# Seven more weight pairs in the Strassen-like form, with even and odd tiles as its halves and the sums over x made ahead

## What is computed

```python
x = x + 0.5 * swiglu_ffn(rms_norm(x, norm_g[i, 0]), ffn_w_gu[i, 0], ffn_w_down[i, 0])
h = rms_norm(x, norm_g[i, 1])
...
x = x + 0.5 * swiglu_ffn(rms_norm(x, norm_g[i, 2]), ffn_w_gu[i, 1], ffn_w_down[i, 1])
```

## Time and profile before

| | us |
|---|---|
| runs of the kernel | 2163.83, 2163.85, 2165.5; median 2163.85 |
| the profiled execution | 2163.63 |
| its span, first to last instruction | 2161.8 |
| TensorE busy | 2144.5 |
| VectorE busy | 1680.9 |
| ScalarE busy | 1176.7 |
| GpSimd busy | 253.0 |

### The profile page before, as it was taken

The page is one execution under the profiler, slowest core; times in us unless marked ns, Lnnn a source line. Parts: engine busy times, 40 slices in busy tenths (PEclk is TensorE's granted clock), DMA queues, the critical chain, the costliest instruction groups (busy, mean ns, idle before and its releaser), DMA issues.

```text
span 2161.8 us, 33546 instructions
## 1 busy us (share of the span) xinstructions
PE 2144.5 (99%) x13412; PEld 1835.3 (85%) x13412; DVE 1680.9 (78%) x2546; ACT 1176.7 (54%) x1922; POOL 253.0 (12%) x187
## 2 busy tenths in 40 slices
PE   9999999999999999999999999999999999999999
PEld 6989897777779898989899997777789898977777
DVE  8789697988678796888787787777688886966873
ACT  6536264667556263546355356777555362638672
POOL 3000004000040000040010112000130000030000
PEclk9999999999999999999999999999999999999999
DMA  7454535131135555354554542222135545332211
GB/s 214 123 136 99 151 94 161 40 98 60 46 89 141 124 137 151 84 162 125 176 129 127 122 126 92 77 75 95 50 79 150 137 100 150 98 131 74 79 59 39
DMA packets 249451, 237.75 MB, mean 110 GB/s; under 512 B 4984, under 2 KB 245240, under 8 KB 249296
## 3 DMA queue, kind: packets, MB, share of 16 engines
q1 hardware_dynamic: 208336, 210.25, 30.3%
q0 software_dynamic: 40752, 25.11, 8.7%
q10 hardware_dynamic: 208, 0.24, 0.0%
HBM read 213.79 MB, written 6.32 MB: 102 GB/s over the span
## 4 chain that ended last, share of the span: by engine, by line
PE 91%; DVE 4%; ACT 2%; issue 1%; DMA 0%; SPq 0%; ACTq 0%; DVEq 0%
PE ps L1982 90%; PE ps L1986 1%; DVE sb_wlo L1334 1%; DMA sb_raw<-ffn_w_gu 0%; ACT sb_whi L771 0%; DVE sb_gla_ek L1689 0%; DVE sb_gla_eq L1692 0%; ACT sb_hyb_th L771 0%; ACT sb_lnb L771 0%; DVE sb_gla_cf L1681 0%; DVE sb_gla_xb L1684 0%; DVE sb_gla_d L1669 0%; SPq L737 0%; DVE sb_rb L1965 0%; ACT sb_xh L771 0%
## 5 line engine op out<-in xcount | busy, mean ns | idle before, releaser
L1982 PE MATMUL ps<-sb_xh,sb_whi 128*128 128x512 f32 (+1 forms) x1812 | 625.4, 345 | 3.6 <-issue 1.8
L1982 PE MATMUL ps<-sb_xl,sb_whi 128*128 128x512 f32 (+1 forms) x1812 | 608.8, 337 | 0.1
L1982 PE MATMUL ps<-sb_xh,sb_wlo 128*128 128x512 f32 (+1 forms) x1812 | 606.7, 337 | 0.0
L771 ACT ACTIVATE sb_whi<-sb_raw 128x1024 fp32r<-128x1024 f32 (+1 forms) x368 | 379.9, 1037 | 376.6 <-PE ps L1982 359.8
L1982 PEld LDWEIGHTS ps<-sb_xh,sb_whi 128*128 128x128 f32 x1812 | 344.0, 190 | 56.8 <-issue 20.4
L1982 PEld LDWEIGHTS ps<-sb_xl,sb_whi 128*128 128x128 f32 x1812 | 344.2, 190 | 39.3 <-DVE sb_xl L1354 3.3
L1982 PEld LDWEIGHTS ps<-sb_xh,sb_wlo 128*128 128x128 f32 x1812 | 343.9, 190 | 37.1
L1982 PE MATMUL ps<-sb_ffn_tl,sb_whi 128*128 128x256 f32 x1200 | 339.6, 283 | 0.0
L1982 PE MATMUL ps<-sb_ffn_th,sb_whi 128*128 128x256 f32 x1200 | 339.6, 283 | 0.0
L1982 PE MATMUL ps<-sb_ffn_th,sb_wlo 128*128 128x256 f32 x1200 | 339.6, 283 | 0.0
L1334 DVE TENSOR_TENSOR sb_wlo<-sb_raw,sb_whi 128x1024 fp32r<-128x1024 f32 (+1 forms) x218 | 275.6, 1271 | 49.1 <-ACT sb_whi L771 48.6
(11 more groups left out here) (293 smaller groups left out, 2919.9 us busy)
## 6 DMA issues: line engine op xcount, KB each, us to landing
sb_raw<-ffn_w_gu SPq DMA_DIRECT2D x86, 1024.0 KB, 5.8
sb_raw<-ffn_w_down SPq DMA_DIRECT2D x32, 1024.0 KB, 5.1
sb_raw<-sb_raw POOLq DMA_DIRECT2D x75, 256.0 KB, 4.2
sb_raw<-w_ada SPq DMA_DIRECT2D x12, 1024.0 KB, 7.6
sb_raw<-ffn_w_down SPq DMA_DIRECT2D x16, 768.0 KB, 5.6
sb_raw<-gla_w_in SPq DMA_DIRECT2D x12, 1024.0 KB, 5.5
sb_raw<-diff_w_in SPq DMA_DIRECT2D x12, 1024.0 KB, 5.1
sb_raw<-w_in SPq DMA_DIRECT2D x10, 1024.0 KB, 5.1
```

The costliest lines, as they stand in the source:

```text
L771: return e.activation(out, in_, func, bias=bias, scale=scale)
L1982: return e.matmul(out, lhsT, rhs, start=start, stop=stop, skip_group_check=skip)
```

## The change

It makes the fourth pair of FFN one fast, and the second and third pairs of the other FFNs (`FAST` from 3, and from 1). The halves of the contraction are no longer tiles 0 to 3 and 4 to 7 but the even and the odd tiles, so that a group t of the sums needs tiles 2t and 2t + 1 of x alone. `scaled_x` and `high_sums` become `high_step`, `x_sums` and `low_sums` become `low_step`. In FFN two to four the groups 0, 1 and 2 are made in the stage before, behind the tiles that `SUMS_AHEAD` names (tiles 5, 5 and 6 of the output projections; tiles 3, 5 and 7 of FFN two's last down projection), the fourth at pair 0. The scaled tiles are written where the gates lie later. In FFN two to four the norm's factor and the plain pair's gate, SiLU and product are now handled inside the first fast pair. GpSimd adds gate onto up for that pair before its last squares.

```diff
-FAST = (tuple(range(4, 22)),) + (tuple(range(3, 22)),) * 3
-SUMS_AT = (((), (0, 1), (2, 3), ()),) + (((0, 1), (2, 3), ()),) * 3
+FAST = (tuple(range(3, 22)),) + (tuple(range(1, 22)),) * 3
+SUMS_AT = (((), (0, 1), (2, 3), ()),) + (((3,), ()),) * 3
+SUMS_AHEAD = ((), (5, 5, 6), (3, 5, 7), (5, 5, 6))
 SCALE_FROM = (2, 1, 1, 1)
 RING_FROM = (0, 0, 5, 0)
-RING_SKIP = (2, 2, 2, 3)
+RING_SKIP = (1, 0, 0, 1)
```

ScalarE in a fast pair:

```diff
+                            if j == SCALE_FROM[f]:
+                                norm_factor(NORM_OF_FFN[f], FFN_NORM)
+                            if i == fast_before[f]:
+                                w.wait_ge(sem["t_vec"], low_sums_done(f, 3))
                             w.wait_ge(sem["t_prod"], 3 * i + 1)
                             if i >= 2:
                                 w.wait_ge(sem["f_join"], 2 * i - 3)
                             act(one_v[i % 2][:, 0, :], run[:, 0:256], ACT.Copy).then_inc(sem["t_cap"], 1)
+                            if j == SCALE_FROM[f]:
+                                silu(0)
                             if j > k0:
                                 split(j - 1)
                             w_hi(u + 1)
```

ScalarE in the last down projection, behind `x_hi`, and its new function:

```diff
+                        if last and f == 1 and m in SUMS_AHEAD[2]:
+                            high_step(2, SUMS_AHEAD[2].index(m))
...
+            def high_step(f, t):
+
+                y, th = ffn_mem[f][2], ffn_mem[f][6]
                 if t:
                     w.wait_ge(sem["t_vec"], x_sums_done(f, t - 1))
                 for k in range(2):
+                    act(y[k], x[:, 2 * t + k, :], ACT.Copy,
+                        scale=col("norm_g", NORM_OF_FFN[f] * KT + 2 * t + k)).then_inc(sem["t_act"], 1)
+                for n in {0: (), 3: (2, 3)}.get(t, (t - 1,)):
+                    w.wait_ge(sem["t_vec"], x_sums_done(f, n))
+                    act(th[:, n, :, :], x_out[f][n % 2], ACT.Copy).then_inc(sem["t_act"], 1)
```

ScalarE in an output projection, behind `w_hi`:

```diff
+                    for t in range(3):
+                        if norm is not None and SUMS_AHEAD[2 * n + 1][t] == m:
+                            w.wait_ge(sem["out_x"], n * KT + 2 * t + 2)
+                            high_step(2 * n + 1, t)
```

VectorE in a fast pair:

```diff
                         if j in FAST[f]:
+                            if j == SCALE_FROM[f]:
+                                plain_gate(0, u - 2)
+                                product(0, u - 2)
                             w_lo(u + 1)
```

VectorE in the last down projection, behind the tile's add, and its new function:

```diff
+                        if last and f == 1 and m in SUMS_AHEAD[2]:
+                            low_step(2, SUMS_AHEAD[2].index(m))
                         if last and f < 3 and m == KT - 1:
                             x_lo(NORM_OF_FFN[f] + 1, m)
...
+            def low_step(f, t):
+
+                th, tl = ffn_mem[f][6:8]
+                x_sums(f, t)
+                for n in {0: (), 3: (2, 3)}.get(t, (t - 1,)):
+                    w.wait_ge(sem["t_act"], high_sums_done(f, n))
+                    e.tensor_tensor(tl[:, n, :, :], x_out[f][n % 2], th[:, n, :, :].bitcast(F32),
+                                    ALU.subtract).then_inc(sem["t_vec"], 1)
```

VectorE in an output projection, before the tile's add:

```diff
+                    for t in range(3):
+                        if norm is not None and SUMS_AHEAD[2 * n + 1][t] == m:
+                            low_step(2 * n + 1, t)
                     used(w, u)
```

TensorE in a fast pair (its other five products change their tiles likewise):

```diff
-                product(run, slots[0], 0, of_x(0, early), 0, True, False).then_inc(sem["t_prod"], 1)
-                product(two, slots[0], 4, of_x(4, early), 4, True, True).then_inc(sem["w_used"], 1)
+                product(run, slots[0], even, of_x(0, early), 0, True, False).then_inc(sem["t_prod"], 1)
+                product(two, slots[0], odd, of_x(1, early), 1, True, True).then_inc(sem["w_used"], 1)
```

GpSimd in `ffn_squares` and `out_squares`, before the squares of tile m:

```diff
+                    if f == 1 and m == 6:
+                        gate_onto_up(2, 1)
...
+                    if m == 5:
+                        gate_onto_up(2 * n + 1, 1)
```

More of the change, by code:

```diff
@@ L446, in ffn_memory @@
             one_v = [ov[:, 2 * i:2 * i + 2, :] for i in range(2)]
-            x_out[f] = x_sum[f][:, 4:8, :], ov[:, :, :]
+            x_out[f] = first_out[:, :, :], ov[:, :, :]
             four_five = sb(f"ffn{f}_ff", [128, 2, 256], F32, mem)
-            gate = [sb(f"ffn{f}_g{i}", [128, S], F32, mem) for i in range(2)]
+            gates = sb(f"ffn{f}_g", [128, 2, S], F32, mem)
+            x_sum[f] = gates[:, :, :].rearrange("p k (c d) -> p (k c) d", d=256)
             up = [sb(f"ffn{f}_u{i}", [128, S], F32, mem) for i in range(2)]
@@ L452, in ffn_memory @@
             th, tl = (sb(f"ffn{f}_{n}", [128, 4, 4, 256], F32R, mem) for n in ("th", "tl"))
-            return ah, al, [g[:, :] for g in gate], up, (one_v, four_five), sums, th, tl
+            return ah, al, tiles_of(gates), up, (one_v, four_five), sums, th, tl
         ffn_mem = []
@@ L1342, in weight_sums @@
                     w.wait_ge(sem[f"raw{q % NRAW}"], 16 * (q // NRAW + 1))
-                a_, b_ = (raw[gate % NRAW][:, k:k + 4, off:off + 128] for k in (0, 4))
-                c_, d_ = (raw[up % NRAW][:, k:k + 4, off:off + 128] for k in (0, 4))
+                a_, b_ = (raw[gate % NRAW][:, k:KT:2, off:off + 128] for k in (0, 1))
+                c_, d_ = (raw[up % NRAW][:, k:KT:2, off:off + 128] for k in (0, 1))
                 lo_done(w, u - 1)
@@ L1419, in ffn @@
                         w_lo(u)
+                        if J == 48:
+                            lambda_products()
                         if f == 1 and j == 4:
@@ L2110, in fast_pair, with product @@
                 early, late = slice(0, 256), slice(256, 512)
-                def product(out, slot, t0, parts, ready, start, stop):
-                    for t in range(4):
-                        if ready is not None:
-                            w.wait_ge(sem["x_lo"], 8 * NORM_OF_FFN[f] + ready + t + 1)
+                def product(out, slot, tiles, parts, odd, start, stop):
+                    for t, k in enumerate(tiles):
+                        if odd is not None:
+                            w.wait_ge(sem["x_lo"], 8 * NORM_OF_FFN[f] + 2 * t + odd + 1)
                         else:
@@ L2118, in product, with of_x @@
                         hi, lo = parts(t)
-                        mm(out, whi[slot][:, t0 + t, :], hi, start and t == 0, False, True)
-                        mm(out, whi[slot][:, t0 + t, :], lo, False, False, True)
-                        ins = mm(out, wlo[slot][:, t0 + t, :], hi, False, stop and t == 3, True)
-                    return ins
-                def of_x(k0, half):
-                    return lambda t: (xh[:, k0 + t, half], xl[:, k0 + t, half])
+                        mm(out, whi[slot][:, k, :], hi, start and t == 0, False, True)
+                        mm(out, whi[slot][:, k, :], lo, False, False, True)
+                        ins = mm(out, wlo[slot][:, k, :], hi, False, stop and t == 3, True)
+                    return ins
+                def of_x(odd, half):
+                    return lambda t: (xh[:, 2 * t + odd, half], xl[:, 2 * t + odd, half])
                 def of_sums(k):
@@ L2599, in gate_onto_up @@
                         w.wait_ge(sem["s_add"], 3 * i - 3)
-                    e.dma_start(raw[up % NRAW][:, 0:4, off:off + 128], raw[gate % NRAW][:, 0:4, off:off + 128],
+                    e.dma_start(raw[up % NRAW][:, 0:KT:2, off:off + 128], raw[gate % NRAW][:, 0:KT:2, off:off + 128],
                                 accum_op=ALU.add).then_inc(sem[f"s_pre{i % 2}"], 16)
             def gates_onto_ups(f):
-                for j in FAST[f]:
+                for j in FAST[f][f > 0:]:
                     gate_onto_up(f, j)
```

41 lines of the change are left out of this document (11 added, 30 removed).

## The result

| | before | after |
|---|---|---|
| median of the runs, us | 2163.84 (2163.82 to 2165.5, 4 runs) | 2199.86 (2198.79 to 2200.26, 4 runs) |
| the profiled execution | 2163.63 | 2198.79 |
| its span | 2161.8 | 2197.0 |

The ratio is 1.0164, with a 95% interval of 1.0146 to 1.0181: 36 us slower. The forecast was 21 us slower (2185), with a range that ended at 2196.

What follows compares the result with a forecast made beforehand. TensorE, busy 2144.5 of 2161.8 us, was taken to bound the kernel. FFN one +1.5, two +6.0, three +8.0, four +5.5 summed to +21: span 2182.8, forecast 2185 us, 1.0% slower; range 2171 to 2196.

Steps and rivals of the forecast that it cites:

- Rival (a): No new wait: VectorE's idle time in the output projection takes the work; -5.7, 2158 us; chance 0.06.
- (b): Gains and waits nearly cancel, with undisturbed durations and a short ScalarE chain: 2164 to 2167 us; chance 0.07.
- (d): Undisturbed waits throughout, VectorE not slowed beside GpSimd: +10, 2174 us; chance 0.14.
- I take 5.0: FFN two's first pair: TensorE waits 5.0 us for VectorE's low part of x's tile 0, behind the moved sums.
- FFN four's 4.6: FFN four's first pair: same VectorE queue after the other output projection, wait taken as 4.6 us, bounds 1.6 and 5.8.
- the bound of 5.8: FFN two's first-pair wait with VectorE's operations lengthened by GpSimd; the undisturbed chain gave 1.6 us.
- FFN three, 8.3: FFN three's first pair: 8.3 us of waits before tiles 6 and 7, from sums and ScalarE round trips.
- bounds of 5.4 and 12: FFN three's first-pair wait: 5.4 us undisturbed throughout, 12 with no relief.
- Rival (c): Forecast waits plus the clock falling in three long stalls, say 2 us each: +6, 2191 us; chance 0.18.
- The lower bound, "nothing": Clock cost of a stall: nothing, since the clock stayed at 1.00 after FFN one's 1.81 us wait.
- The wait in the first fast pair, 2.6, 1.3 and 2.5: FFN two, three, four: TensorE waits these us for ScalarE's copy of the second partial result.
- FFN one, +1.5: Chain before the fourth pair moves by 1.8 us, copy 0.5 late, less 0.8 saved: +1.5 us net.

Runs made afterwards that it cites:

- e5: The change, but GpSimd squares and adds one column of x's tiles 1 to 7 instead of 512; 2170.73 us, ratio 1.003.
- e1: The change's even and odd halves alone, with fast pairs, times of the sums and ring offsets of the kernel before; 2163.9 us, ratio 1.0001.
- e7: The change, but at FFN two's last down projection's last tile VectorE makes x's last low part before group 2's sums and group 1's low part; 2197.08 us.
- e6: The change, plus extra matmuls into an unread bank that fill TensorE's waits in FFN two to four; 2195.89 us, ratio 1.0145.
- e4: The change with its 82 fast pairs but no sums ahead, all four groups at pair 0 of FFN two to four; 2207.92 us, ratio 1.0202.
- c1: c0 with the third pair of FFN two, three and four also fast, no sums ahead; 2179.18 us, ratio 1.007.
- d1: c1 with the order of the kernel before (sums ahead of factor, SiLU and product) in FFN two to four; 2173.38 us, ratio 1.0044.
- e2: e1 with FFN one's fourth pair also fast; 2166.85 us, ratio 1.0012.
- c2: c0 with FFN one's fourth pair also fast; 2167.36 us, ratio 1.0015.
- c0: The kernel before, with factor, SiLU and products of the waiting pairs ahead of the sums at that pair; 2161.71 us, ratio 0.9987.
- e3: The change's sums made ahead, but with the fast pairs of the kernel before; 2189.92 us, ratio 1.0117.

## Why the prediction was off

**The direction and the places held.** VectorE's queue in front of x's first low part, the two waits in FFN three, ScalarE's copy in the first fast pair, the longer wait in FFN one: each stands in the trace with the releaser that was named. Rival (a), no new wait, and (b), nearly nothing, are out, and so is (d): undisturbed durations hold only when GpSimd is made nearly idle (e5). The pairs save what was reckoned (80.63 us for eight), and the halves cost nothing (e1).

**Two steps failed. The first: FFN two's first pair, "I take 5.0", and FFN four's 4.6.** They measured 8.0 and 8.8, beyond even the bound of 5.8. The bound was no bound: it put 1.0 us of GpSimd's disturbance on a group's sums (0.7 on group 2's in its chain, against its own words) and took the weight sums nearly as undisturbed (2.4 us for three). Group 0's took 4.1 us rather than 2.5 (in FFN four 4.4), group 2's 3.0, the weight sums 3.8. Group 1's (1.6) and the weight's low part behind tile 5's add (1.2) had nothing beside them and were shorter than the bound had them. Then I took less than my own chain, because "GpSimd will be less dense": but its operations did fall beside VectorE's new ones, each of which has two inputs in SBUF. What I had in hand were the 2.17 us of one operation of 1.2, about 1 us more for one operation; I spread that 1 us over the three of a group instead of giving it to each. e5 shows the size: GpSimd's part is 6.7 and 7.5 us.

The Trainium skill ("SBUF — State Buffer", "SBUF: two separate sides") says that a VectorE operation with two inputs in SBUF and a GpSimd operation that reads SBUF hold the shared port pair for the whole instruction each, the other blocked. The trace agrees: operations of 0.42 us measured 1.40 and 1.15 beside GpSimd. By that rule an estimate of one GpSimd operation (1.04 us at 605.80) in front of each of VectorE's gives 1.5 + 3.1 = 4.6 us for group 0, near the 4.1 measured. Put on all three groups and on the weight sums it would have given a wait of some 15 us, further off than the 5.0: what had to be reckoned was which operations meet.

**FFN three, 8.3 against 9.8.** The three round trips of 2.0 us were right. The part taken off for relief was somewhat too large; the weight sums beside GpSimd (1.41 and 1.75) weren't in it. (The bounds of 5.4 and 12 there are given without their steps and can't be redone from the text.) The part before tile 7 isn't GpSimd's (5.2 us in e5), it is the order (1.0 in e7).

**The second, and the larger: the clock, which the sum had at nothing; the slow matmuls behind the waits measured 9.3 us.** Rival (c) was the right mechanism, with a price of 2 against 2.4 measured, but it was set apart as a case of 18 in 100, for three waits. For the waits that the forecast itself had, it was no question of chance: after the idle times of 3.71, 4.59, 4.69, 7.79 and 8.62 us the granted clock was at 0.50 to 0.61, in FFN one too, and it fell behind every wait of 2.4 us and more in all the profiles here. e6 shows that idleness is the cause. The lower bound, "nothing", rested on the one wait of 1.81 us behind which the clock stayed at 1.00 (the windows of the earlier trace rows lie elsewhere; 46.40:51.00, shown with e1, is the one that says so). e1 shows that even a wait of that size can cost 1.6 us. The other bound, 3.1 from the kernel's first ten matmuls, took them to run at half pace, which no row shows: the granted clock is given as 1.00 in all of the kernel's first 8 us. That "say 2" came near the 2.4 was luck. The Trainium skill's rule ("TensorE: Matmul & The Clock Gate", "What's actually happening") that an idle TensorE falls back to 1.2 GHz agrees with these rows, and stood in the prediction. The forecast with the clock in it reads 2191 at rival (c)'s price for three waits and 2194 at the measured one for all, both inside the range; the waits as measured, less the 3 us of the first fast pairs, bring it to the result.

**The wait in the first fast pair, 2.6, 1.3 and 2.5 against 1.09 three times.** ScalarE's timeline after:

```profile
636.60 0.63 ACT L774 ACTIVATE sb_whi<-sb_ffn_sums 128x512 fp32r<-128x512 f32 x1 [0.98 <-PE ps L2000]
...
640.04 1.28 ACT L774 ACT_TABLE_LOAD   x1
...
644.28 0.36 ACT L774 ACTIVATE sb_ffn_ff<-ps 128x256 f32<-128x256 f32 x1
```

The chain is the one that was written down, in its order. From the end of the pair (637.3) to the end of the copy (644.6) it is 7.3 us, not 8.1: the first high part starts at 636.60, 0.7 us before the pair's end, and not at it. The addition for "pushed late" in two and four was wrong as well. The length of the first-pair waits has no part in it: in e5, where they are 1.3, 5.2 and 1.3 us, this wait is the same 0.93 in all three FFNs.

**FFN one, +1.5 against +2.7.** The wait grew by 1.9, near the 1.8 of the chain; the 0.5 for the copy inside the fast pair didn't come. The slow matmuls' 1.6 were missing.

**What would beat both kernels** is not an earlier fast pair. In the four ways tried (the change, e4, c1, d1) and in FFN one's two (e2, c2) the 0.81 us of a pair cost more than that. The groups of sums came late in e4, c1 and c2; that no other order would find them room isn't shown. c0 keeps before's pairs and wins 2.1 us by its order alone. A kernel with the sums ahead and GpSimd's squares on another engine, or made earlier, wasn't tried; e5, which leaves the squares out nearly wholly, is still 7 us slower than before.

## What to carry to other kernels

Before work is moved ahead of a stage, add up the queue of the engine that feeds the stage's first operation, operation by operation, at the durations that it has beside its neighbour, not in a quiet stretch; where GpSimd runs in the same stretch, each VectorE operation with two SBUF inputs can take 1 us more. A long wait of TensorE carries the clock's price with it (in these profiles 1.6 to 2.8 us behind each single wait of 2.4 us and more, 2.9 to 3.5 behind FFN three's two, and 1.6 behind two of the four single ones of 1.8 and 1.9): add it to the sum, not to the rivals. A change that saves 0.8 us per step and lengthens a busy queue has to be hidden wholly, or it loses.

## What the runs showed of the hardware that was not expected

- The same wait can cost nothing or 1.6 us: behind FFN one's 1.8 us the clock stayed at 1.00 in the profiles of before and e3 and fell to 0.50 in e1's. Behind FFN one's 3.7 us the slow matmuls came to 1.6 us in the change, e2 and e4, 2.6 in e7 and 2.8 in e6.
- The fall needn't come with the wait. After an idle time of 3.71 us (FFN one) the third matmul was already slow. After 3.60 us in d1 12 matmuls came first at full pace (0.12 us), then 16 at 0.21. Windows of d1:

```profile
637.70:639.30 1.60, 1.52 (x12) 1.52 (x13) 0.28 (x2) 1.24 (x2) 0.00 (x0) 1.00 0.00 0
639.30:642.50 3.20, 3.20 (x17) 3.20 (x16) 2.58 (x5) 2.73 (x5) 0.00 (x0) 0.50 0.00 0
```

- Several short idle times in a row were followed by the low clock as well: in c2, after 1.02, 0.58 and 1.86 us, the granted clock of the next 2 us was 0.52.
- Of two operations beside each other the one that started later took longer in these rows: VectorE's of 618.05 kept its 0.68 us, and GpSimd's, 0.16 us later, took 1.42 instead of 1.04. A VectorE operation of 0.42 us took up to 1.40 beside GpSimd (3.3 times), one of 0.69 up to 1.78 (FFN four), while ScalarE's scaling of two tiles took 1.32 to 1.34 us in both kernels, beside GpSimd too.
